# Turning the residual stream before its norm weights are applied: layer 0's embedding norm and layer 1's attention norm of a two-layer decoder trunk

## The reference, cut to what matters

```
for i in 0, 1:
    h = rms_norm(x, attn_norm[i])
    x = x + attention_mixers(h @ w_in[i], ...) @ w_out[i]
    h = rms_norm(x, ffn_norm[i])
    x = x + (swiglu(h) if i == 0 else moe_swiglu(h))
    h = rms_norm(x, ple_norm[i])                                  # the "embedding norm"
    x = x + sigmoid(h @ ple_w_gate[i]) * (p[i] @ ple_w_proj[i])
out = rms_norm(x, final_norm)

rms_norm(x, g) = x / sqrt(mean(x*x) + 1e-6) * g                   # g has one value per column of x
```

## Time and profile before

| | |
|---|---|
| median of three runs | 1851.56 us (1850.57 to 1852.08) |
| the profiled execution: its own time | 1851.78 us |
| its span, first to last instruction | 1850.0 us |
| mean granted TensorE clock | 0.995 of 2.4 GHz |
| PE, DVE, ACT, POOL busy | 99%, 80%, 67%, 7% of the span |

### The profile page before, as it was taken

One profiled execution on the slowest core, in us unless ns is written; L12 is line 12 of the kernel. 1 busy time (PEld: TensorE's weight loads), 2 busy tenths in 40 slices (PEclk: granted clock), 3 DMA queues, 4 the chain that ended last, 5 costly groups with the idle time before them and its releaser, 6 DMA issues.

```text
span 1850.0 us, 27386 instructions
## 1 busy us (share of the span) xinstructions
PE 1824.5 (99%) x8982; PEld 1526.7 (83%) x8982; DVE 1471.1 (80%) x1692; ACT 1246.3 (67%) x1571; POOL 132.0 (7%) x200
## 2 busy tenths in 40 slices
PE   8999999999999999999999999999999999999997
PEld 7888888888888888887888888888888888888886
DVE  5556776665676556777999999999999999999997
ACT  5555655444455555656778788888887877878885
POOL 1300000000002100001200101001001010010000
PEclk9999999999999999998999999999999999999999
DMA  8543235555546543346999999999999999999992
GB/s 335 211 175 120 92 143 194 184 190 192 183 172 237 205 145 109 112 143 257 375 384 373 388 368 383 382 370 391 364 386 376 373 391 364 393 382 361 411 377 91
DMA packets 74033, 512.57 MB, mean 277 GB/s; under 512 B 8256, under 2 KB 8256, under 8 KB 14064
## 3 DMA queue, kind: packets, MB, share of 16 engines
q1 hardware_dynamic: 69232, 494.76, 69.4%
q0 software_dynamic: 4736, 16.95, 3.2%
HBM read 502.76 MB, written 8.91 MB: 277 GB/s over the span
## 4 chain that ended last, share of the span: by engine, by line
PE 95%; DVE 2%; issue 1%; ACT 1%; POOL 1%; DMA 0%; DVEq 0%; POOLq 0%; SPq 0%; ACTq 0%
PE ps L1788 28%; PE ps L1795 28%; PE ps L1789 28%; PE ps L1964 2%; PE ps L2211 1%; PE ps L1946 1%; PE ps L1921 1%; PE ps L1897 1%; PE ps L1907 1%; PE ps L1806 1%; PE ps L1831 1%; DVE lo L1144 0%; PE ps L1808 0%; PE ps L1812 0%; PE ps L1957 0%
## 5 line engine op out<-in xcount | busy, mean ns | idle before, releaser
L1144 DVE TENSOR_TENSOR lo<-raw,hi 128x1024 fp32r<-128x1024 f32 (+1 forms) x940 | 1100.3, 1211 | 187.9 <-ACT hi L678 184.7
L678 ACT ACTIVATE hi<-raw 128x1024 fp32r<-128x1024 f32 (+1 forms) x940 | 968.8, 1050 | 320.2 <-PE ps L1795 303.5
L1788 PE MATMUL ps<-hi,hs_hi 128*128 128x512 f32 x896 | 356.3, 398 | 0.0
L1789 PE MATMUL ps<-hi,hs_lo 128*128 128x512 f32 x896 | 350.1, 391 | 0.0
L1788 PE MATMUL ps<-hi,hT_hi 128*128 128x512 f32 (+1 forms) x784 | 307.9, 394 | 1.5 <-ACT hi L678 0.6
L1789 PE MATMUL ps<-hi,hT_lo 128*128 128x512 f32 (+1 forms) x784 | 301.3, 386 | 0.0
L1795 PE MATMUL ps<-lo,hs_hi 128*128 128x512 f32 x896 | 276.9, 390 | 1.1 <-DVE lo L1144 1.1
L1795 PE MATMUL ps<-lo,hT_hi 128*128 128x512 f32 (+1 forms) x784 | 206.1, 386 | 0.6 <-DVE lo L1144 0.6
L1795 PEld LDWEIGHTS ps<-lo,hs_hi 128*128 128x128 f32 x896 | 168.4, 188 | 37.8 <-DVE lo L1144 1.5
L1788 PEld LDWEIGHTS ps<-hi,hs_hi 128*128 128x128 f32 x896 | 168.9, 189 | 33.4
L1789 PEld LDWEIGHTS ps<-hi,hs_lo 128*128 128x128 f32 x896 | 169.0, 189 | 33.3
(11 more groups left out here) (329 smaller groups left out, 1714.0 us busy)
## 6 DMA issues: line engine op xcount, KB each, us to landing
raw<-in_stream SPq DMA_DIRECT2D x468, 1024.0 KB, 5.4
ybuf<-xs POOLq DMA_DIRECT2D x2, 1024.0 KB, 5.5
xs<-in_x SPq DMA_DIRECT2D x2, 512.0 KB, 5.9
gain<-in_ffn_norm POOLq DMA_DIRECT2D x2, 512.0 KB, 6.9
gain<-in_ple_norm POOLq DMA_DIRECT2D x2, 512.0 KB, 6.1
hbuf<-hnf POOLq DMA_DIRECT2D x1, 1024.0 KB, 4.5
xs<-ybuf POOLq DMA_DIRECT2D x1, 1024.0 KB, 12.6
out_x<-hnat SPq DMA_DIRECT2D x4, 256.0 KB, 2.3
```

The costliest lines, as they stand in the source:

```text
L678: a.activation(dst, src, ACT.Copy).then_inc(hi_done, 1)
L1144: v.tensor_tensor(dst, src, h, ALU.subtract).then_inc(lo_done, 1)
L1788: pe.matmul(o, ah, wh[:, kk, :], start=(first and kk == 0), stop=False)
L1789: pe.matmul(o, al, wh[:, kk, :], start=False, stop=False)
```

## The change

For these two norms the weight vector is no longer multiplied into x before the turn. PE turns x itself, and ACT and DVE apply the weights when they empty the turned banks, where a model column is a partition and the weight is one number per partition: `gcol`, [128, 2, 8], loaded by POOL with one 4-byte piece per element. The turned blocks are laid out by k block, two to a bank, both token blocks side by side, so a round or rest takes 256 columns and there are eight of each in a norm in place of four. ACT scales and rounds (`k_round`); DVE multiplies the bank by the weight and subtracts the rounded half in one operation (`k_rest`). `x_gain` is gone from both norms, and with it a wait of DVE on itself. A turned bank now needs both token blocks of x. The first product after a half waits by k block (`by_k`) instead of for the whole half. The other norms are as before.

```
+        gcol = sb("gcol", [P, 2, KD])
+        def k_bank(k):
+            return ps[:, 4 + k // 2, S * (k % 2):S * (k % 2) + S]
 POOL
+            def load_columns(j, src):
+                g.dma_start(gcol[:, j, :], src.rearrange("(k p) -> p k", p=P)).then_inc(gain_in, 16)
-                load_gain(ple_norm[i])
+                if i == 0:
+                    load_columns(0, ple_norm[0])
+                else:
+                    load_gain(ple_norm[1])
...
-                load_gain(attn_norm[1] if i == 0 else final_norm)
+                if i == 0:
+                    load_columns(1, attn_norm[1])
+                else:
+                    load_gain(final_norm)
 ACT
+            def k_round(n, h, r):
+                a.wait_ge(gain_in, 16 * GAINS.index(n))
+                for j in (2 * h, 2 * h + 1):
+                    a.wait_ge(n.tr, n.g + j + 1)
+                    for k in (2 * j, 2 * j + 1):
+                        ins = a.activation(hT_hi[:, k, :], k_bank(k), ACT.Copy, scale=gcol[:, r, k:k + 1])
+                    ins.then_inc(n.hi, 1)
-            hT_round(n3, 0)
+            k_round(n3, 0, 0)
...
 DVE
+            def k_rest(n, h, r):
+                for j in (2 * h, 2 * h + 1):
+                    v.wait_ge(n.hi, n.g + j + 1)
+                    for k in (2 * j, 2 * j + 1):
+                        ins = v.scalar_tensor_tensor(out=hT_lo[:, k, :], in0=k_bank(k), scalar=gcol[:, r, k:k + 1],
+                                                     in1=hT_hi[:, k, :], op0=ALU.mult, op1=ALU.subtract)
+                    ins.then_inc(n.lo, 1)
-                    v.tensor_tensor(xm, xm, m, ALU.add).then_inc(y.padd, 1)
-                    v.wait_ge(y.padd, 2 * c + t + 1)
-                    x_gain(n, 2 * c + t)
+                    v.tensor_tensor(xm, xm, m, ALU.add).then_inc(n.hn, 1)
...
-                f_add(c, 4 + 2 * c)
-                v.wait_ge(f_xadd, 2 * NF + c)
-                x_gain(n3, 2 * c)
-                x_gain(n3, 2 * c + 1)
+                for t in range(T):
+                    m = xs[:, t, CH * c:CH * c + CH]
+                    v.scalar_tensor_tensor(out=m, in0=ps[:, 4 + 2 * c + t, :], scalar=r2[:, t:t + 1], in1=m,
+                                           op0=ALU.mult, op1=ALU.add).then_inc(n3.hn, 1)
...
 PE
-                    if ready and h % 2 == 0:
-                        pe.wait_ge(ready[0], ready[1] + 2 + h)
+                    if ready:
+                        pe.wait_ge(ready[0], ready[1] + (max(2, 1 + h) if by_k else 2 + h - h % 2))
+            def k_turn(n, h):
+                for j in (2 * h, 2 * h + 1):
+                    pe.wait_ge(n.hn, n.g + 2 * h + 2)
+                    for k in (2 * j, 2 * j + 1):
+                        for t in range(T):
+                            ins = pe.transpose(k_bank(k)[:, P * t:P * t + P], xs[:, t, P * k:P * k + P], ident[:])
+                    ins.then_inc(n.tr, 1)
-                    if k == 4:
-                        pe.wait_ge(y.n1.lo, y.n1.g + 4)
+                    if k in (4, 6):
+                        pe.wait_ge(y.n1.lo, y.n1.g + (4 if i == 0 else 1 + k // 2))
...
```

More of the change, by code:

```diff
@@ L970, in _ @@
             split_to(b + 89)
-            hT_round(n3, 0)
+            k_round(n3, 0, 0)
             square(n3, 1)
             split_to(b + 90)
-            hT_round(n3, 1)
+            k_round(n3, 1, 0)
             g0, n1 = PLG0[0], layers[1].n1
@@ L980, in _ @@
             split_to(g0 + 10)
-            hT_round(n1, 0)
+            k_round(n1, 0, 1)
             split_to(g0 + 11)
@@ L985, in _ @@
             split_to(g0 + 12)
-            hT_round(n1, 1)
+            k_round(n1, 1, 1)
             attn(1)
@@ L1530, in _ @@
                 done(b + 83 + 2 * c)
-                f_add(c, 4 + 2 * c)
-                v.wait_ge(f_xadd, 2 * NF + c)
-                x_gain(n3, 2 * c)
-                x_gain(n3, 2 * c + 1)
+                for t in range(T):
+                    m = xs[:, t, CH * c:CH * c + CH]
+                    v.scalar_tensor_tensor(out=m, in0=ps[:, 4 + 2 * c + t, :], scalar=r2[:, t:t + 1], in1=m,
+                                           op0=ALU.mult, op1=ALU.add).then_inc(n3.hn, 1)
                 if c == 0:
                     split_to(b + 88)
-                    hT_rest(n3, 0)
+                    k_rest(n3, 0, 0)
                     split_to(b + 89)
-            hT_rest(n3, 1)
+            k_rest(n3, 1, 0)
             mean_square(n3)
@@ L1544, in _ @@
             split_to(g0 + 10)
-            hT_rest(n1, 0)
+            k_rest(n1, 0, 1)
             split_to(g0 + 11)
@@ L1548, in _ @@
             split_to(g0 + 12)
-            hT_rest(n1, 1)
+            k_rest(n1, 1, 1)
             mean_square(n1)
@@ L1814, in wide_unit, with cols @@
                 ins.then_inc(used, 1)
-            def cols(u, dyn, l_hi, l_lo, outs, w=CH, nku=2, units=4, ready=None, turn_between=None):
+            def cols(u, dyn, l_hi, l_lo, outs, w=CH, nku=2, units=4, ready=None, turn_between=None, by_k=False):
                 for h in range(units):
-                    if ready and h % 2 == 0:
-                        pe.wait_ge(ready[0], ready[1] + 2 + h)
+                    if ready:
+                        pe.wait_ge(ready[0], ready[1] + (max(2, 1 + h) if by_k else 2 + h - h % 2))
                     if turn_between and h == turn_between[0]:
-                        x_turn(turn_between[1], turn_between[2])
+                        turn_between[3](turn_between[1], turn_between[2])
                     unit(u + h, dyn, l_hi, l_lo, (nku, w), nku * h, outs, 0, h == 0, h == units - 1)
@@ L1847, in attn @@
                             pe.wait_ge(layers[0].pev_vec, 4)
[L1848 to L1850 removed]
+                        (x_turn, k_turn)[i](y.n1, 1)
+                    if k in (4, 6):
+                        pe.wait_ge(y.n1.lo, y.n1.g + (4 if i == 0 else 1 + k // 2))
                     wide_unit(b + U_L + k, dyn, hT_hi, hT_lo, LW, k, (2, 4), k == 0, k == KD - 1)
@@ L2110, in _ @@
             pe.wait_ge(layers[0].ev_vec, 10)
-            cols(b, 0, hT_hi, hT_lo, (0, 1), ready=(n2.lo, n2.g), turn_between=(1, n2, 1))
+            cols(b, 0, hT_hi, hT_lo, (0, 1), ready=(n2.lo, n2.g), turn_between=(1, n2, 1, x_turn))
             ple_turn(0)
@@ L2150, in _ @@
             n3, n1 = layers[0].n3, layers[1].n1
-            cols(b + 84, 0, faT_hi, faT_lo, (6, 7), units=2, turn_between=(1, n3, 0))
+            cols(b + 84, 0, faT_hi, faT_lo, (6, 7), units=2, turn_between=(1, n3, 0, k_turn))
             g0 = PLG0[0]
-            cols(g0, 0, hT_hi, hT_lo, (4, 5), ready=(n3.lo, n3.g), turn_between=(1, n3, 1))
-            cols(g0 + 4, 0, hT_hi, hT_lo, (6, 7), turn_between=(2, n1, 0))
+            cols(g0, 0, hT_hi, hT_lo, (4, 5), ready=(n3.lo, n3.g), turn_between=(1, n3, 1, k_turn), by_k=True)
+            cols(g0 + 4, 0, hT_hi, hT_lo, (6, 7), turn_between=(2, n1, 0, k_turn))
             attn(1)
```

## The result

The changed kernel takes 1873.01 us (median of five runs, 1870.65 to 1875.34) against 1851.56 us before (five runs, 1850.57 to 1852.39). The ratio is 1.0117, with a 95% interval of 1.0106 to 1.0129. The forecast of 1850.1 and its range up to 1852.6 are missed by over 20 us. The profiled execution took 1872.81 us, with a span of 1871.0.

What follows compares the result with a forecast made beforehand. PE, busy 99% of the span, was taken as the bound, losing 2.4 us in the stage. 0.99 + 0.5 = 1.5 us off the median 1851.56 gave 1850.1 (50%); own range 1849.2 to 1851.0, 8 in 10 1848.2 to 1852.6.

Steps and rivals of the forecast that it cites:

- Sum.: Whole kernel: 0.99 from the first norm and 0.5 from the second make 1.5 us off, nothing after the stage changes.
- The part on waits: PE's waits and semaphores: no matmul or turn added or taken away, added `by_k` waits already met when PE arrives.
- ACT's four rounds: Rounds of a half as four 256-column scaled operations: 1.54 us, +0.48 against the two 512-column ones.
- DVE's four rests: Rests of a half as four 256-column three-operand operations: 1.74 us, +0.45 against the two before.
- Before g0: First norm, half 0: longer steps eat the earlier start, so PE's 0.38 us loss stays.
- From g0 to g0+2: First norm, half 1: the turn and g0+2 no longer wait, so the 0.99 us lost there go.
- In the second norm: Half 1, fourth and fifth wide units: of 0.97 us lost, 0.5 go and 0.5 stay in another place.
- The waits by k block: First norm, before g0+2: they hide 0.15 us that waiting for the whole half would cost.
- Rivals 1 and 2: All of the stall goes, 1849.2 us, 14%; or nothing goes or small pieces cost more, 1851.6 to 1852.4, 24%.
- rival 3: The `gcol` column load lands late and DVE stands at `ple_gate`: +15.8 - 1.5, 1866 us, 4%.
- a second low clock: Another stretch at granted clock 0.50, like that after layer 1's router: 1855 us, 2%.
- Rival 4: The low clock after layer 1's router moves: 1845.1 us without it, 6%; 1855 with a second, 2%.

Runs made afterwards that it cites:

- The run with the changed order: Changed kernel with `gcol` last, ACT rounding the first half before a split, ACT and DVE splitting between the last half's banks: 1848.08 us, ratio 0.9985.
- the pad: Changed kernel with `gcol` in its place and 192 unused bytes behind it, so regions move by 256 in all: 1848.82 us, ratio 0.9986.
- the two mended kernels: Changed kernel with `gcol` behind all other tiles, 1849.04 us, and changed kernel with 192 unused bytes behind `gcol`, 1848.82 us.

## Why the prediction was wrong

**The step that failed** is "**Sum.** 0.99 + 0.5 = 1.5 us off, 0 for the rest", with its reason, "Nothing after the stage takes it back: PE stays the bound through the experts". PE did stay the bound, and just for that every nanosecond on its products counts. The diff's first added line, the declaration of `gcol`, got no term at all: the 64 bytes were taken as free, and which tiles lie behind them was not looked at. The shift costs 2688 x 5.1 ns on `hs` (13.7 us), 1344 x 6.1 on `eaT` (8.2) and 336 x 5.9 on `faT` (2.0): 23.9 us. The kernel before with the shift alone was 23.7 slower, and its profiled execution too had the shorter low clock. The starts of the changed kernel give about the same: 2.4 in layer 0 (2.2 of them in the feed-forward), 0.3 in layer 1's attention and 19.9 and 1.2 in and behind the experts are some 23.9 us longer. The stage is 1.5 shorter, the low clock at the router took 1.6 less, 0.2 lie ahead of all this, and the last matmul comes 21.0 later. The part on waits says "No matmul and no turn is added or taken away", which is true, and from it I wrongly concluded that the matmuls cost what they did.

**The steps inside the stage held**, nearly all in size too.
- ACT's four rounds take 1.55 us where 1.54 was taken, DVE's four rests 1.66 where 1.74 was. ACT and DVE after, in the first norm:

```profile
532.97 1.06 ACT L692 ACTIVATE hi<-raw 128x1024 fp32r<-128x1024 f32 x1 [0.50 <-PE ps L1825]
533.93 1.55 ACT L730 ACTIVATE hT_hi<-ps,gcol 128x256 fp32r<-128x256 f32 x4
```

```profile
534.79 1.66 DVE L1226 SCALAR_TENSOR_TENSOR hT_lo<-ps,gcol,hT_hi 128x256 fp32r<-128x256 f32 x4 [0.93 <-ACT hT_hi L730]
```

- Before g0, 0.38 us were to stay (the steps given for it end at 533.91, not at 533.87 as written). The rests end at 534.79 + 1.66 = 536.45 and g0 starts at 536.50. Counted from 536.61 against 532.71 + 0.87 + 2.72 = 536.30 it is 0.31, some 0.07 of which is the slower pace of the `faT` unit in between.
- From g0 to g0+2 nearly all of the 0.99 went: 536.61 to 542.99 is 6.38, for 6.31.
- In the second norm 0.5 of 0.97 was to stay, before the fifth wide unit. PE's timeline after, beside the earlier trace rows:

```profile
565.73 1.03 PE L1870 MATMUL ps<-ident,xs 128*128 128x128 f32 x8
566.52 0.55 PE L1836 MATMUL ps<-hi,hT_hi 128*128 128x336 f32 x2
...
568.79 0.55 PE L1836 MATMUL ps<-hi,hT_hi 128*128 128x336 f32 x2 [0.19 <-ACT hi L692]
...
570.77 0.47 PE L1836 MATMUL ps<-hi,hT_hi 128*128 128x336 f32 x2
```

The fourth unit follows its turn at once; the fifth was due at 565.73 + 0.87 + 1.84 = 568.44 and counts from 568.90, 0.46 lost. The sixth starts 1.87 after that, so that 0.03 at most are DVE's. The working had 0.3 for ACT's split and 0.2 for DVE's rest: the sum came out, its parts did not. ACT's split stands behind the round, as forecast:

```profile
566.42 1.57 ACT L730 ACTIVATE hT_hi<-ps,gcol 128x256 fp32r<-128x256 f32 x4 [0.71 <-PE ps L1870]
567.87 2.75 ACT L692 ACTIVATE hi<-raw 128x672 fp32r<-128x672 f32 x4
```

The run with the changed order takes both these losses away: g0 starts 0.05 us after its due time, the fifth wide unit at it. So the orders are shown to be the cause, in the second norm ACT's and DVE's together.
- The waits by k block hide 0.44, where 0.15 was taken, and in the second norm rather than at g0+2.

**The rivals.** Rivals 1 and 2 are out: the stage is neither 42.7 nor 45. Two cases lay on the right side, rival 3 (the late load) with 1866 and a second low clock with 1855, with 4% and 2%, and neither is what happened. The load was asked for at 539.20, landed 3.2 us later, and nobody waited for it.

```profile
gcol<-in_ple_norm POOLq DMA_DIRECT2D x1, 4.0 KB, 6.4
gcol<-in_attn_norm POOLq DMA_DIRECT2D x1, 4.0 KB, 3.2
```

(The Trainium skill, "DMA: Bandwidth & Descriptors", section "Rules for kernel authors", advises against one descriptor per element. Here it cost the path nothing: with 1024 of them the load was back at about 543, and DVE first asked for it behind the split that ended at 548.3.)

Rival 4, the low clock that moves, is real. Before, the clock was low for 10.2 us from 850.0 on the earlier trace rows. The changed kernel, whose clock has this window on the way down,

```profile
853.00:855.00 2.00, 2.00 (x14) 2.00 (x13) 1.53 (x2) 2.00 (x4) 1.79 (x5) 0.60 0.54 223
```

had 6.8 us of it, from 853.4 on. In both PE had stood still shortly before, with 2.0 and 1.8 us between two starts. The kernel with `gcol` last had the same 1.8 and no low clock behind it:

```profile
848.00:850.00 2.00, 0.85 (x8) 0.85 (x8) 1.93 (x6) 2.00 (x3) 0.00 (x0) 1.00 0.53 217
850.00:852.00 2.00, 2.00 (x21) 2.00 (x20) 0.76 (x2) 2.00 (x4) 1.40 (x3) 1.00 0.12 37
```

From matmul 4350 to 4500 the three traces take 34.10, 32.52 and 29.60 us, so the low clock costs up to 4.5. My ground against it, that the runs agree, held for the kernel before alone. The faster versions fall into groups: with the pad three of eleven runs are at 1846.6 to 1846.8, seven at 1848.8 to 1849.4, one at 1851.7, with mean clocks of 0.998, 0.996 to 0.997, and 0.995. What decides between 10.2, 6.8 and 0 us was not tried. (The Trainium skill, "TensorE: Matmul & The Clock Gate", section "What's actually happening", calls the activity window free-running. Groups within one kernel agree with that; that this is the cause is not shown.) So of the 2.3 to 2.8 us that the two mended kernels gain by their medians, 1.5 is the stage, shown by window in each of them; the rest has the size of what this clock makes, but is not shown to be it execution by execution.

**What stays open**: why the place relative to the ring matters. Shown are offsets modulo 256 of 0 (fast), 64 and 128 (slow), for products of 512 fp32r columns with a 128x128 tile in the array, both out of the same memory. ACT and DVE are not needed for it. Offsets under 64, other forms, and which of PE's two reads gives way were not tried.

## What to carry to other kernels

A new tile is part of a change even at 64 bytes: list the addresses of what lies behind it before and after, and put small additions behind everything else. Where PE is the bound, keep what stands in the array and what streams through it at the same place modulo 256 per partition, and measure it. If the span grows while PE stays 99% busy and no wait grew, compare the start-to-start distance of one matmul form by tile: the busy share cannot show a slower pace.

## What the runs showed of the hardware that was not expected

- A 512-column product takes 227 to 228 ns from start to start when its stationary tile lies at the weight ring's place modulo 256, and 233 when it lies 64 or 128 off, 2.2 to 2.8% more. Moving both together changes nothing.
- After a gap of about 2 us in PE's work the traces of three kernels show 10.2, 6.8 and 0 us at a granted clock of 0.50. Executions of one kernel differ too: eleven with the pad have mean clocks from 0.995 to 0.998, and times 5.2 us apart.
- 1024 pieces of 4 bytes landed in 3.2 and 6.4 us, no more than the 256 pieces of the earlier trace rows took with 7.0.
